# Latent attention: the query projections moved next to the key selection, the index logits ordered by head

## The reference, cut to what matters

```python
proj = h @ w_in                          # 1024 -> q 16x64, ckv 256, iq 8x64, ik 64, iw 8
q, ckv, iq, ik, iw = jnp.split(proj, A_SPLITS, axis=-1)
ckv = _rms_norm(ckv, kv_norm)
# per block of 128 queries:
idx_logits = einsum('bqhd,bsd->bhqs', iqb, ik)
score = einsum('bhqs,bqh->bqs', relu(idx_logits), iwb)     # sum over the 8 index heads
score = where(causal, score, -inf)
_, sel = top_k(score, 128)
q_lat = einsum('bqhd,hdr->bqhr', qb, w_uk) * 64 ** -0.5
logits = einsum('bqhr,bqkr->bhqk', q_lat, ckv[sel]) + rel_bias[bucket(tpos - sel)]
p = softmax(where(valid, logits, NEG))
o = einsum('bqhr,hrd->bqhd', einsum('bhqk,bqkr->bqhr', p, ckv[sel]), w_uv)
```

## Time and profile before

| | us |
|---|---|
| three timed runs, median (lowest to highest) | 3735.73 (3731.39 to 3739.24) |
| the profiled execution's own time | 3738.83 |
| its span in the trace | 3737.2 |
| TensorE matmuls busy | 3270.3 (88%) |
| VectorE busy | 1493.1 (40%) |
| ScalarE busy | 569.1 (15%) |
| DMA traffic | 562.94 MB, mean 151 GB/s |

### The profile page before, as it was taken

One profiled execution on the slowest core, in us unless ns is written; L12 is line 12 of the kernel. 1 busy time (PEld: TensorE's weight loads), 2 busy tenths in 40 slices (PEclk: granted clock), 3 DMA queues, 4 the chain that ended last, 5 costly groups with the idle time before them and its releaser, 6 DMA issues.

```text
span 3737.2 us, 38054 instructions
## 1 busy us (share of the span) xinstructions
PE 3270.3 (88%) x11721; PEld 1672.5 (45%) x11722; DVE 1493.1 (40%) x3389; ACT 569.1 (15%) x1263; POOL 245.3 (7%) x317
## 2 busy tenths in 40 slices
PE   3999898869999678797999374989999899899998
PEld 2445555544444543232333242544444466454443
DVE  6545464545665733242443647541100433420003
ACT  1001112210000111121222122421000133210000
POOL 1000000001110320000000300000000000000000
PEclk9989999978999779998999687989999999899999
DMA  7553213117775249999896711312121124032110
GB/s 244 164 185 102 68 57 101 40 31 228 224 233 175 113 176 398 360 380 362 333 372 240 248 40 29 124 60 93 68 90 62 45 68 135 23 107 90 68 68 23
DMA packets 260291, 562.94 MB, mean 151 GB/s; under 512 B 21113, under 2 KB 156820, under 8 KB 234586
## 3 DMA queue, kind: packets, MB, share of 16 engines
q1 hardware_dynamic: 212570, 397.16, 30.1%
q0 software_dynamic: 40128, 137.19, 10.8%
q10 hardware_dynamic: 7488, 27.27, 1.8%
HBM read 513.24 MB, written 52.50 MB: 151 GB/s over the span
## 4 chain that ended last, share of the span: by engine, by line
PE 73%; DVE 11%; issue 4%; ACT 2%; DMA 2%; POOL 1%; SPq 1%; DVEq 0%; ACTq 0%; POOLq 0%
PE ps L1445 11%; PE ps L1153 9%; PE ps L1460 9%; PE ps L1029 5%; PE ps L950 5%; PE ps L1282 4%; PE ps L1174 4%; PE ps L1053 3%; PE ps L1038 3%; PE ps L1471 3%; PE ps L957 2%; PE ps L1307 2%; PE ps L1316 1%; PE ps L1140 1%; DMA WR<-in_w_up 1%
## 5 line engine op out<-in xcount | busy, mean ns | idle before, releaser
L1153 PE MATMUL ps<-WR,hT 128*64 x832 | 391.1, 626 | 72.6 <-DVEq L2306 41.1
L1445 PE MATMUL ps<-hT,WR 128*128 128x512 f32 x960 | 412.3, 592 | 0.0
L1154 PE MATMUL ps<-WR,hT 128*64 128x512 f32 x832 | 391.1, 626 | 0.0
L1460 PE MATMUL ps<-WR 128*128 128x512 f32 x768 | 329.9, 592 | 0.0
L1445 PEld LDWEIGHTS ps<-hT,WR 128*128 128x128 f32 x960 | 182.2, 190 | 228.6 <-issue 228.6
L1153 PEld LDWEIGHTS ps<-WR,hT 128*64 128x64 f32 x832 | 118.6, 144 | 329.6 <-issue 329.6
L2303 DVE COPY WR<-WR 128x1024 f32 x208 | 130.6, 692 | 253.5 <-SPq L594 200.1
L950 PE MATMUL ps<-hT,WR 128*128 128x512 f32 x512 | 229.4, 603 | 1.7 <-DVEq L2004 1.7
L1460 PEld LDWEIGHTS ps<-WR 128*128 128x128 f32 x768 | 145.9, 190 | 183.7 <-issue 183.7
L1906 DVE SCALAR_TENSOR_TENSOR WR<-xr,csil,WR 128x256 f32<-128x256 f32 x448 | 217.2, 485 | 16.0
L2151 DVE TENSOR_TENSOR WR<-ps,grow 128x1024 f32<-128x1024 f32 x20 | 24.5, 1223 | 433.1 <-PE ps L1471 369.2
(11 more groups left out here) (365 smaller groups left out, 4166.4 us busy)
## 6 DMA issues: line engine op xcount, KB each, us to landing
WR<-in_w_gate SPq DMA_DIRECT2D x64, 1024.0 KB, 9.8
WR<-in_w_up SPq DMA_DIRECT2D x64, 1024.0 KB, 12.0
WR<-in_w_down SPq DMA_DIRECT2D x64, 1024.0 KB, 10.3
WR<-in_mlp_w SPq DMA_DIRECT2D x32, 2048.0 KB, 7.8
xr<-in_ada_w POOLq DMA_DIRECT2D x48, 1024.0 KB, 5.8
WR<-in_w_in SPq DMA_DIRECT2D x56, 512.0 KB, 6.4
xr<-in_w_ada POOLq DMA_DIRECT2D x16, 1024.0 KB, 5.8
WR<-in_w_in SPq DMA_DIRECT2D x16, 1024.0 KB, 5.4
```

Source lines behind the costliest of these rows:

```text
L1153: mm(out[0:HALF], xT[u][:, k, 0:HALF], wa[:, :, k, :], start=(k == 0), stop=(k == KD - 1))
L1154: last = mm(out[HALF:P], xT[u][:, k, HALF:P], wb[:, :, k, :], start=(k == 0), stop=(k == KD - 1))
L1445: last = mm(ps[:, n % 8, :], w[:, k, j * P:(j + 1) * P], hT[:, k, :], start=(k == 0), stop=(k == KD - 1))
L1460: last = mm(ps[:, 2 * t + n, :], h1T[:, k, t * P:(t + 1) * P], w[:, k - 4 * u, 512 * n:512 * n + 512], start=(k == 0), stop=False)
```

## The change

All eight query projections leave the attention loop. They are done in the index stage and during the key selection and kept in `oT[:, g]`, where the output of the same pair is written later. Their weights come as two units of 512 columns (`dsa_q`, slots 0 and 1); w_uk and w_uv of all pairs come as one unit (`dsa`, slot 2, 3 DMAs), so the loop has no fills. The later stages take slots one further on, and `residual` frees the slot of the stage that ran last.

The scores go by head (three blocks per head), through two PSUM banks instead of four. They start at the third index query projection: `project_with_scores` puts one score behind each of the first six matmuls of the projections index 2 and 3, query 0 and 1. Projections alternate between banks 4 and 5, and each waits for ScalarE's copy of the one before the last. The latent's transposes stand behind the third index projection. ScalarE's and VectorE's orders follow. In a turn of the loop the values are split in two halves, which stand where the later parts of the query projection stood.

```diff
-INDEX_P = dict(ckv_p=1, iw_p=2, iq_p=3, ckv_T=6)
-INDEX_A = dict(ckv_sq=1, iqk=6, ckvn=6 + TT, ckvT=8 + TT)
+INDEX_P = dict(ckv_p=1, iw_p=2, iq_p=[3, 4, 5], ckv_T=6, q_p=6)
+INDEX_A = dict(ckv_sq=1, ik=2, iq=[3, 4, 5 + TT, 8 + TT], ckvn=4 + TT, ckvT=7 + TT, q=8 + TT)
+SCORES = (TT - 1) * 8
...
-    ("dsa", 4, [(0, 4), (1, 4)]),
-    ("a_w_o", 1, [(2, 1), (3, 1)]),
+    ("dsa_q", 1, [(0, 1), (1, 1)]),
+    ("dsa", 1, [(2, 3)]),
+    ("a_w_o", 1, [(3, 1), (0, 1)]),
...
+            for u in range(2):
+                fill("dsa_q", u, 0, (unit("dsa_q", u, 0, KD, 512), a_w_in[:, :, u * 512:u * 512 + 512]))
+            fill("dsa", 0, 0, (unit("dsa", 0, 0, HEADS // 2, KV_RANK), w_uk),
+                 *[(unit("dsa", 0, 2048 + 1024 * r, HEADS, HEAD), w_uv[:, r, :, :]) for r in range(2)])
...
+            def score(n):
+                h, qb = n // (TT - 1), n % (TT - 1) + 1
+                half = slice(64 * (h % 2), 64 * (h % 2) + 64)
+                if qb == 1:
+                    pe.wait_ge(sem("index_a"), INDEX_A["iq"][h // 2])
+                pe.wait_ge(sem("idx_free"), n + 1)
+                mm(ps[:, 6 + n % 2, 0:(qb + 1) * P], iqT[half, h // 2, qb * P:(qb + 1) * P],
+                   ikT[half, 0:(qb + 1) * P], start=True, stop=True).then_inc(sem("idx_p"), 1)
+
+            def project_with_scores(out, w, at):
+                for k in range(KD):
+                    last = mm(out, w[:, k, :], hT[:, k, :], start=(k == 0), stop=(k == KD - 1))
+                    if at is not None and k < 2 * (TT - 1):
+                        score(at + k)
+                return last
...
+            for g in range(HEADS // 2):
+                u, j = g // 4, g % 4
+                if j == 0:
+                    have("dsa_q", u)
+                if g < 2:
+                    pe.wait_ge(sem("index_a"), INDEX_A["iq"][2 + g])
+                else:
+                    pe.wait_ge(sem("index_a"), INDEX_A["q"] + g - 1)
+                last = project_with_scores(ps[:, 4 + g % 2, :], unit("dsa_q", u, 0, KD, 512)[:, :, j * P:(j + 1) * P],
+                                           2 * (TT - 1) * (2 + g) if g < 2 else None)
+                last.then_inc(sem("index_p"), 1)
+                if j == 3:
+                    pe.wait_ge(sem("index_p"), INDEX_P["q_p"] + g + 1)
+                    pe.sem_inc(used[ring.slot("dsa_q", u)], 1)
...
                 def logits(qb, c, par):
                     if qb == 0:
-                        pe.wait_ge(sem("att_qkv"), c * 3 + 2 + past["qkv"])
+                        pe.wait_ge(sem("att_qkv"), c * each + (each - 1) + past["qkv"])
+                        if dsa:
+                            pe.wait_ge(sem("index_a"), INDEX_A["q"] + c + 1)
+                    q_in = oT[:, c, :] if dsa else qkv[par][:, 0, :]
...
                         if dsa:
-                            project(q_out, par, 0, 2, 5)
+                            latent_values(p, 0, 2)
...
                         if dsa:
-                            project(q_out, par, 0, 5, KD).then_inc(sem("att_proj"), 1)
-                        values(par)
+                            latent_values(p, 2, TT)
+                        else:
+                            values(par)
...
+            index_q(0)
+            index_q(1)
             act.wait_ge(sem("ckv_rstd"), 1)
             for t in range(TT):
                 v = ps[:, t // 2, (t % 2) * KV_RANK:(t % 2 + 1) * KV_RANK]
                 A(ckvn[:, t, :], v, ACT.Copy, scale=rstd[:, t:t + 1]).then_inc(sem("index_a"), 1)
+            scored(0)
+            scored(1)
+            index_q(2)
...
+            for g in range(1, HEADS // 2):
+                query(g)
...
-                            ("idx_free", 4), ("idx_s", 2),
+                            ("idx_free", 2), ("idx_s", 2),
...
-                            dve.sem_inc(used[3], 1)
+                            dve.sem_inc(used[ring.slot(*last_weights[n])], 1)
...
-            for qb in range(1, TT):
+            for n in range(SCORES):
+                h, qb = n // (TT - 1), n % (TT - 1) + 1
                 w = (qb + 1) * P
                 score = selm[:, qb, 0:w]
```

More of the change, by code:

```diff
@@ L257, in program @@
         a_w_in = a["a_w_in_2"][0].rearrange("(k p) n -> p k n", p=P)
-        w_uk = a["a_w_uk_2"][0].rearrange("(j h) d r -> j (h d) r", h=2)
+        w_uk = a["a_w_uk_2"][0].rearrange("(j h) d r -> (h d) j r", h=2)
         w_uv = a["a_w_uv_2"][0].rearrange("h (k p) d -> p k h d", p=P)
@@ L1245, in _ @@
             for j in range(4):
-                for k in range(KD):
-                    last = mm(ps[:, 4 + j, :], w[:, k, j * P:(j + 1) * P], hT[:, k, :],
-                              start=(k == 0), stop=(k == KD - 1))
+                if j >= 2:
+                    pe.wait_ge(sem("index_a"), INDEX_A["iq"][j - 2])
+                last = project_with_scores(ps[:, 4 + j % 2, :], w[:, :, j * P:(j + 1) * P],
+                                           2 * (TT - 1) * (j - 2) if j >= 2 else None)
@@ L1249, in _ @@
                 if j < 3:
                     last.then_inc(sem("index_p"), 1)
[L1251 to L1259, removed]
@@ L1260, in _ @@
-            n = 0
-            for qb in range(1, TT):
[L1262 to L1268, removed]
+                else:
+                    spent(last, "index", 1)
@@ L1276, in attention @@
                 per = 8 if dsa else 4
+                each = 2 if dsa else 3
                 q_out, k_out, v_out = ps[:, 5, :], ps[:, 6, :], ps[:, 7, :]
@@ L1295, in latent_keys, with latent_values @@
                     last.then_inc(sem("att_proj"), 1)
+                def latent_values(p, lo, hi):
+                    w = unit(tag, 0, 2048, 2, 1024)[:, :, p * P:(p + 1) * P]
+                    for t in range(lo, hi):
+                        q = slice(t * P, (t + 1) * P)
+                        for r in range(2):
+                            last = mm(v_out[:, q], ckvT[:, r, q], w[:, r, :], start=(r == 0), stop=(r == 1))
+                    if hi == TT:
+                        last.then_inc(sem("att_proj"), 1)
                 def values(par):
+                    w = unit(tag, par, 2048, KD, P)
                     for t in range(TT):
                         q = slice(t * P, (t + 1) * P)
[L1300 to L1307, removed]
+                        for kk in range(KD):
+                            last = mm(v_out[:, q], hT[:, kk, q], w[:, kk, :], start=(kk == 0), stop=(kk == KD - 1))
                     last.then_inc(sem("att_proj"), 1)
@@ L1355, in turn_of @@
                     if p is not None:
-                        have(tag, par, turn)
                         if dsa:
-                            turn_uk(p, par)
-                        project(q_out, par, 0, 0, 2 if dsa else 4)
+                            if p == 0:
+                                have(tag, 0)
+                            turn_uk(p)
+                        else:
+                            have(tag, par, turn)
+                            project(q_out, par, 0, 0, 4)
                     if f is not None:
@@ L1363, in turn_of @@
                         logits(1, c, 1 - par)
-                        pe.wait_ge(sem("att_qkv"), c * 3 + 3 + past["qkv"])
-                        pe.sem_inc(used[1 - par], 1)
+                        pe.wait_ge(sem("att_qkv"), c * each + each + past["qkv"])
+                        if not dsa:
+                            pe.sem_inc(used[ring.slot(tag, 1 - par)], 1)
+                        elif p is None:
+                            pe.sem_inc(used[ring.slot(tag, 0)], 1)
                     if p is not None:
@@ L1701, in _ @@
                 A(ckvT[:, r, :], ps[:, r, :], ACT.Copy, scale=kv_norm[:, r:r + 1]).then_inc(sem("index_a"), 1)
-            n = 0
-            for qb in range(1, TT):
-                for h in range(IDX_HEADS):
-                    act.wait_ge(sem("idx_p"), n + 1)
-                    act.wait_ge(sem("idx_s"), n + 1)
-                    A(rl[:, n % 2, 0:(qb + 1) * P], ps[:, 4 + n % 4, 0:(qb + 1) * P],
-                      ACT.Relu).then_inc(sem("idx_free"), 1)
-                    n += 1
-            act.wait_ge(sem("idx_s"), 2 + n)
+            scored(2)
+            scored(3)
+            index_q(3)
+            scored(4)
+            scored(5)
+            query(0)
+            scored(6)
+            scored(7)
+            for g in range(1, HEADS // 2):
+                query(g)
+            act.wait_ge(sem("idx_s"), 2 + SCORES)
             def attention(tag):
@@ L1722, in projected @@
                 def projected(n, nth, p, par):
-                    act.wait_ge(sem("att_proj"), p * 3 + nth + past["proj"])
+                    act.wait_ge(sem("att_proj"), p * each + nth + past["proj"])
                     A(qkv[par][:, n, :], ps[:, 5 + n, :], ACT.Copy).then_inc(sem("att_qkv"), 1)
```

76 lines of the change are left out of this document (41 added, 35 removed).

## The result

The changed kernel's median is 3744.94 us over 18 runs (3740.30 to 3747.81), the one before 3737.73 us over 18 (3731.39 to 3743.42): ratio 1.0019, 95% interval 1.0011 to 1.0026. It is slower by 7.2 us; the forecast was 3734. The time lies inside the range of 3721 to 3749, but the sign of the change is wrong, and the interval excludes no change at all, though the prediction took 0.2% to be the least that this measurement can tell. The profiled execution took 3744.51 us, span 3742.9 (before 3738.83 and 3737.2), so the two traces differ by 5.7 us and can be compared stage by stage.

The account below looks back on a forecast made before the run. VectorE was taken to bound the key selection and TensorE the attention loop; loads +2, selection +7.2, first pair's turn -1.3 and six turns -9.3 gave net -1.4 us, forecast 3734 us, range 3721 to 3749.

Parts of the forecast that it names:

- the price of a score: Index stage: 24 threaded scores take 15.2 us of TensorE, the price of scores among scores; no row showed it between full-array matmuls.
- the later selection: Index stage: VectorE's key selection starts 7.2 us later, bounds 0 to 10, 57.7 us after the first index query matmul.
- rival 2: Attention loop: the clock falls twice a turn, turn 20.6 us instead of 19.65, total 3749 us; chance 0.17.
- Loads: Gathers before the index stage: 2.5 MB more weight traffic delays them by 2 us, bounds 0 to 6.7.
- Hidden queries: Key selection: the moved query projections fit into TensorE's idle time, busy about 46 of 62 us, last 16 empty.
- Rival 4: Key selection: the hole is too small to hide the moved queries; given no chance.
- First pair's turn: First attention turn after the selection: 15.5 us instead of 16.89, a gain of 1.3 us.
- second pause: TensorE's 2.6 us idle before a turn's last transposes; clock falls after it in seven turns of ten, at 1.9 us.
- Six turns: Attention loop: each turn 18.1 us instead of 19.65, clock falls included, a gain of 9.3 us over six.
- first pause: TensorE's 1.7 us idle earlier in a turn; clock falls after it in two turns of ten, at 1.6 us.
- Rival 1: Attention loop: the clock holds at 1.00, turn 16.5 us, net -11, total 3725 us; chance 0.24.
- Tail: The last pair's tail after the six turns: unchanged, since it has no projection in it before the change either.

Follow-up runs that it names:

- full-row kernel: The changed kernel with every score matmul over all 128 rows, the index key kept twice with zeros in one half; 3732.44 us, ratio 0.9987 to the kernel before.
- pauses filled: The changed kernel with unread 512-column matmuls in the loop's pauses, one in the first and two in the second; 3734.44 us, ratio 0.9996 to the kernel before.
- second pause filled: The changed kernel with two unread matmuls before each turn's last transposes and none in the first pause; 3736.65 us, ratio 0.9996 to the kernel before.
- scores in twos: The changed kernel with two scores behind every second projection matmul instead of one behind each; 3735.26 us, ratio 0.9992 to the kernel before.
- queries-alone kernel: The kernel before with only the query projections moved, scores still by block in four banks after all index projections; 3724.67 us, ratio 0.9958 to the kernel before.
- scores-first kernel: The changed kernel with all scores, by head in two banks, after the index projections and before the queries; 3737.20 us, ratio 1.0001 to the kernel before.

## Why the prediction was wrong

The step that failed is the price of a score in the index stage, and with it the term of the later selection: forecast +7.2 us with bounds 0 to 10, measured +16.3. The prediction said that no row shows what a score costs between full-array matmuls, and took the price of scores among scores. Its upper bound asked only what the lost overlap of the halves costs; that a change between heights costs on both sides, the score's and the projection matmul's, was not in it. The full-row kernel puts 66.8 back to 57.6, and 57.7 was forecast: the rest of that term, added up, was right. That the time still lies inside the range is luck: its upper end came from rival 2, whose second fall of the clock did not happen.

- Loads, +2 forecast: 0. The longest gather wait is 8.55 us on VectorE and the traffic 376 GB/s where it was 372, but from the shared down projection to the index queries it is 126.62 us as before (126.5 to 127.5 in the kernels of the experiments, so at most 0.9). The Trainium skill (DMA: Bandwidth & Descriptors, Queues, rings and completion order) says that an engine alternates between queues by the packet. The prediction made 6.7 us of it, and the runs show no such delay.
- Hidden queries: right. TensorE is busy 46.69 us of the selection (forecast 46), and the last 14 are empty (16). Rival 4 falls.
- First pair's turn, -1.3 forecast: -0.3, at clock 0.81 where it was 0.87. With the pauses filled this turn is 15.97 us: 0.6 of the missing 1.0 is a fall of the clock after its own second pause, which the prediction priced in the six turns only.
- Six turns, -9.3 forecast: -9.1. Turn 18.13 (18.1), granted clock 0.91 (0.85 to 0.9), warm turn 16.68 (16.5), second pause 2.51 (2.6). The parts are right except that the first pause never took the clock, and that a fall after the second costs more: 8.7 us for four falls, 2.2 each instead of 1.9, or 1.45 us a turn instead of the 1.6 for both. The two errors offset each other, so part of this nearness is luck. Rival 1 falls: the clock does not hold by itself. So does rival 2, which needs two falls a turn. The rule on clock swings cited from the Trainium skill (TensorE: Matmul & The Clock Gate, A second HAM failure mode: psum-queue depth-cycling) agrees in kind, not in degree: the clock falls in four turns of six and not in every one, and in none with the second pause filled.
- Tail, 0 forecast: -0.6.
- Forecast net -1.4, measured in the traces +5.7. The difference is +9.1 for the scores' price, -2.8 for the start of the index stage, +1.0 for the first pair's turn, +0.2 for the six turns, -0.6 for the tail and 0.2 elsewhere.

Open: what decides whether a given turn loses the clock. The mean turn of kernels without fillers lies between 17.19 (scores in twos) and 18.21 us, and nothing in their loops differs; of six second pauses two to four are followed by the half clock. The full-row kernel's six turns took 106.07 us instead of 108.80, which is part of why it gained more than its 9.2 us in front of the selection.

## What to carry to other kernels

Before interleaving small matmuls with large ones on TensorE, compare how many rows of the array each uses: every change between 64 and 128 rows costs a weight load that is otherwise covered, 0.19 us for these float32 matmuls, so bring them to one height (zeros in the other half cost no time) or group them. Work taken off the engine that bounds a loop leaves pauses; look what the longest does to the clock, and compare with useless matmuls in it before you give up the rest of the gain. When a change has two parts, time the parts: here one gained some 15 us and the other lost some 22 (12 and 17 by the traces).

## What the runs showed of the hardware

- A matmul of 64 rows behind one of 128, or the other way round, starts 0.19 to 0.2 us late, with its weight load beside it instead of ahead. The Trainium skill (TensorE: Matmul & The Clock Gate, Step-by-step: what each phase is for) says that a load is pulled ahead of matmuls in flight when the row groups don't conflict or when it goes to the background buffer. The trace agrees for neighbours of 128 rows (load at 2200.80, matmul at 2201.01); it shows that a change of height loses this.
- Two float32 matmuls on different halves of the array run at once: 512 and 256 columns in 1.05 us together, change included. In the queries-alone kernel the first four scores, 256 columns each and in alternating halves, take 1.14 us instead of 4 x 0.43.
- In the scores-first kernel the clock stays at 0.50 while TensorE is busy 8.94 us of 10, with a wait of 0.5 to 0.7 us in each head.
- A pause of 2.51 us in a turn of 17 us is followed by 0.50 in four of six turns, one of 1.44 us in none of these six, nor in the six of the kernel that has only the second pause filled.
